# A transformer kernel: where the norm's spread, four lots of copies and a scaled product stand in their engines' queues

## What is computed

```python
mem_n = rmsnorm(mem, mem_norm)                       # 256 memory rows
for i in range(2):
    h = rmsnorm(x, norm_mix[i])                      # the mixer's norm
    ...                                              # projections, convolution or banded attention, memory attention
    x = x + concatenate([y_tok, y_mem]) @ w_out
    h = rmsnorm(x, norm_ffn[i])
    x = x + (silu(h @ w_gate[i]) * (h @ w_up[i])) @ w_down[i]
x = rmsnorm(x, final_norm)
...
kc = compress_blocks(k_c, ...); vc = compress_blocks(v_c, ...)   # blocks of 32 positions, stride 16, plus a place table
y_a = (o_a * silu(z_n)) @ w_nsa_o
y_b = (o_b * silu(z_r)) @ w_ret_o                    # o_b: retention, 4 heads, each normalised
merged = sigmoid(m_a) * y_a + sigmoid(m_b) * y_b
x = x + rms_norm(merged @ w_out, norm_post)
```

## Time and profile before

| | us |
|---|---|
| median of 3 runs | 1700.69 |
| lowest, highest | 1699.10, 1703.64 |
| the profiled execution | 1700.62 |
| its span | 1698.8 |
| PE busy in the span | 1634.9 |
| DVE, ACT, POOL busy | 871.4, 571.6, 152.9 |

### The profile page before, as it was taken

How to read it: one execution, slowest core, us unless ns; L and a number is a source line. 1 busy time by engine, 2 the same in 40 slices (tenths; PEclk the granted TensorE clock), 3 DMA queues, 4 the chain that set the end, 5 groups by cost and what they waited for, 6 DMA issues and landing times.

```text
span 1698.8 us, 20511 instructions
## 1 busy us (share of the span) xinstructions
PE 1634.9 (96%) x7720; PEld 1301.2 (77%) x7720; DVE 871.4 (51%) x1106; ACT 571.6 (34%) x962; POOL 152.9 (9%) x139
## 2 busy tenths in 40 slices
PE   7989999999999999879999999999999999999997
PEld 5867878888888876557888888887677777778886
DVE  5565544444423457655444443337476655446443
ACT  5332332222322335533222232322345542234222
POOL 3100100000000102120000001113211001000001
PEclk9999999999999999999999999999999999999999
DMA  5312622232332321122322232242111110232221
GB/s 211 125 62 88 142 89 98 99 97 90 120 102 97 103 71 35 33 73 97 99 99 96 91 125 85 97 186 89 51 63 50 50 63 31 75 98 95 99 100 74
DMA packets 44622, 154.88 MB, mean 91 GB/s; under 512 B 5230, under 2 KB 9999, under 8 KB 44047
## 3 DMA queue, kind: packets, MB, share of 16 engines
q1 hardware_dynamic: 40594, 146.92, 25.7%
q10 hardware_dynamic: 3964, 7.11, 1.9%
HBM read 149.55 MB, written 4.45 MB: 91 GB/s over the span
## 4 chain that ended last, share of the span: by engine, by line
PE 86%; DVE 8%; ACT 3%; issue 2%; POOL 1%; DMA 0%; DVEq 0%; SPq 0%; ACTq 0%; POOLq 0%
PE ps L1741 25%; PE ps L1743 24%; PE ps L1742 24%; DVE w_lo L1064 2%; PE ps L2095 1%; PE ps L2109 1%; PE ps L2131 1%; PE ps L2155 1%; POOL acc L590 1%; ACT w_hi L694 1%; PE ps L2196 1%; PE ps L2195 1%; PE ps L2194 1%; PE ps L1916 1%; DVE a_lo L1069 1%
## 5 line engine op out<-in xcount | busy, mean ns | idle before, releaser
L1741 PE MATMUL ps<-a_hi,w_hi 128*128 128x512 f32 (+1 forms) x1368 | 547.0, 400 | 16.4 <-DVE a_lo L1069 8.3
L1743 PE MATMUL ps<-a_hi,w_lo 128*128 128x512 f32 (+1 forms) x1368 | 535.0, 391 | 0.0
L1742 PE MATMUL ps<-a_lo,w_hi 128*128 128x512 f32 (+1 forms) x1368 | 534.8, 391 | 0.0
L1064 DVE TENSOR_TENSOR w_lo<-raw,w_hi 128x1024 fp32r<-128x1024 f32 (+4 forms) x262 | 324.2, 1237 | 253.6 <-ACT w_hi L694 248.5
L694 ACT ACTIVATE w_hi<-raw 128x1024 fp32r<-128x1024 f32 (+4 forms) x262 | 274.2, 1047 | 268.5 <-PE ps L1743 244.1
L1741 PEld LDWEIGHTS ps<-a_hi,w_hi 128*128 128x128 f32 (+1 forms) x1368 | 257.4, 188 | 82.0 <-issue 16.4
L1743 PEld LDWEIGHTS ps<-a_hi,w_lo 128*128 128x128 f32 (+1 forms) x1368 | 257.2, 188 | 55.8
L1742 PEld LDWEIGHTS ps<-a_lo,w_hi 128*128 128x128 f32 (+1 forms) x1368 | 257.6, 188 | 53.3 <-issue 1.9
L1090 DVE TENSOR_TENSOR tmp<-ps,rstd 128x512 f32<-128x512 f32 x121 | 83.4, 691 | 160.0 <-PE ps L1743 149.8
L1741 PE MATMUL ps<-g_hi,w_hi 128*128 128x512 f32 x352 | 136.9, 389 | 0.0
L1742 PE MATMUL ps<-g_lo,w_hi 128*128 128x512 f32 x352 | 136.9, 389 | 0.0
(11 more groups left out here) (271 smaller groups left out, 1749.4 us busy)
## 6 DMA issues: line engine op xcount, KB each, us to landing
raw<-w SPq DMA_DIRECT2D x135, 512.0 KB, 3.5
raw<-w8b SPq DMA_DIRECT2D x70, 512.0 KB, 3.5
raw<-w_down SPq DMA_DIRECT2D x32, 704.0 KB, 4.0
w<-cmp_w SPq DMA_DIRECT2D x2, 2048.0 KB, 10.9
raw<-w_out_first SPq DMA_DIRECT2D x8, 320.0 KB, 2.8
rel_scratch<-table ACTq DMA_DIRECT2D x1, 2298.0 KB
raw<-w_nsa_o SPq DMA_DIRECT2D x8, 256.0 KB, 2.5
out<-o_t SPq DMA_DIRECT2D x4, 512.0 KB, 2.7
```

Source lines behind the costliest of these rows:

```text
L1064: dve.tensor_tensor(w_lo[:, slot, 0:w], raw[:, raw_slot, 0:w], w_hi[:, slot, 0:w].bitcast(F32), ALU.subtract).then_inc(w_lo_ready, 1)
L1741: pe.matmul(o, wh, a_h, start=start and at == 0, stop=False)
L1742: pe.matmul(o, wh, a_l, start=False, stop=False)
L1743: ins = pe.matmul(o, wl, a_h, start=False, stop=stop and at == kt - 1)
```

## The change

Nothing is computed differently; every engine has the same instructions. What changes is where some of them stand:

- The spread of both mixer norms, of both feed-forward norms and of the memory norm stood ahead of a strip. It is now issued within that strip, behind its fourth tile (12 matmuls).
- On DVE, in both feed-forward layers and in the second mixer, the split's `w_lo` now stands ahead of `diagonal`.
- `windows_of` does four copies at a time, beside strips 188, 189, 190 and 191, in the order values, keys, values, keys.
- At a short strip DVE does `epilogue(n - 1)` ahead of the split (and ahead of the retention statistics), as at every other strip. ACT's order stays.

```diff
@@ vector, ffn @@
                         if first and j == 0:
+                            split(n + 2, w, 0, 2)
                             diagonal(v)
-                            split(n + 2, w, 0, 2)
                             dve.wait_ge(rstd_ready, v + 1)
@@ vector, second mixer @@
                 if n == N_QM1 + 2:
+                    split(n + 1, KT * P)
                     diagonal(V_MIX1)
-                    split(n + 1, KT * P)
                     dve.wait_ge(rstd_ready, V_MIX1 + 1)
@@ vector, third block @@
-            def windows_of(i):
+            def windows_of(i, g):
...
-                for g in range(2):
-                    for odd in range(2):
+                for odd in range(2):
...
-                if n >= N_SECOND + 3 and not short(n):
+                if n >= N_SECOND + 3:
                     epilogue(n - 1)
...
                 if N_SECOND < n < N_END - 1:
                     split(n + 1, width(n + 1))
-                if short(n):
-                    epilogue(n - 1)
...
-                if n in (N_SECOND + 5, N_SECOND + 6):
-                    windows_of(n - N_SECOND - 5)
+                if N_SECOND + 4 <= n < N_SECOND + 8:
+                    windows_of(*((1, 0), (0, 0), (1, 1), (0, 1))[n - N_SECOND - 4])
@@ tensor @@
+            def spread_beside(v, at):
+
+                if at == 3:
+                    spread(v)
...
-                if n == 4:
-                    spread(V_MIX0)
...
-                if n == 9:
-                    spread(V_MEM, 2)
...
-                        strip(n, mem_hi, mem_lo, bank_of(n), cols=NMEM)
+                        strip(n, mem_hi, mem_lo, bank_of(n), cols=NMEM,
+                              aside=(lambda at: spread(V_MEM, 2) if at == 3 else None) if n == 9 else None)
...
-                          aside=(lambda at, n=n: mem_beside(0, n, at)) if n > N_CONV else None)
+                          aside=(lambda at, n=n: mem_beside(0, n, at)) if n > N_CONV
+                          else (lambda at: spread_beside(V_MIX0, at)) if n == 4 else None)
@@ tensor, ffn @@
-                        if first and j == 2:
-                            spread(v)
...
-                              ready=(a_lo_ready, count) if first and j == 0 else None)
+                              ready=(a_lo_ready, count) if first and j == 0 else None,
+                              aside=(lambda at: spread_beside(v, at)) if first and j == 2 else None)
@@ tensor, second mixer @@
             def l1_beside(n, at, last):
+                if n == N_QM1 + 2:
+                    spread_beside(V_MIX1, at)
...
-                if n == N_QM1 + 2:
-                    spread(V_MIX1)
```

More of the change, by code:

```diff
@@ L1425, in windows_of @@
                 dve.wait_ge(small2_in, 16 * 5)
-                for g in range(2):
-                    for odd in range(2):
-                        of, to = slice(HD * g, HD * g + HD), slice(HD * odd, HD * odd + HD)
-                        src = (kcr, vcr)[i][of].rearrange("p (c l o) -> p l c o", l=CSTRIDE // 2, o=2)
-                        for w in range(2):
-                            ls = slice(CSTRIDE // 2 * w, CSTRIDE // 2 * (w + 1))
-                            place = pe2[of, i, odd, ls].unsqueeze(2).to_broadcast([HD, CSTRIDE // 2, NCMP])
-                            dve.tensor_tensor(windows[i][to, ls, g * NCMP:(g + 1) * NCMP],
-                                              src[:, :, w:w + NCMP, odd], place, ALU.add)\
-                                .then_inc(windows_ready, 1)
+                for odd in range(2):
+                    of, to = slice(HD * g, HD * g + HD), slice(HD * odd, HD * odd + HD)
+                    src = (kcr, vcr)[i][of].rearrange("p (c l o) -> p l c o", l=CSTRIDE // 2, o=2)
+                    for w in range(2):
+                        ls = slice(CSTRIDE // 2 * w, CSTRIDE // 2 * (w + 1))
+                        place = pe2[of, i, odd, ls].unsqueeze(2).to_broadcast([HD, CSTRIDE // 2, NCMP])
+                        dve.tensor_tensor(windows[i][to, ls, g * NCMP:(g + 1) * NCMP],
+                                          src[:, :, w:w + NCMP, odd], place, ALU.add)\
+                            .then_inc(windows_ready, 1)
             def cmp_maxima():
```

## The result

| us | before | changed |
|---|---|---|
| median | 1700.69 (1699.05 to 1703.64) | 1708.66 (1705.60 to 1710.61) |
| the profiled execution | 1700.62 | 1710.32 |
| its span | 1698.8 | 1708.5 |

The ratio is 1.0041, with a 95% interval of 1.0029 to 1.0054: 4.9 to 9.2 us slower. I had forecast 1702.5 and a range up to 1706.5. A second set of runs of the same kernel gave 1709.05 and a ratio of 1.0042. One execution in this set (2754.99) and one in another (2417.11, the product with the second mixer) took far longer than all others and are left out of every median here. The kernel before, in the sets of runs that were made beside the experiments, had medians from 1701.7 to 1703.0 (10 to 27 runs each, 1699 to 1705): the three runs shown ahead of the prediction were a little low.

A forecast was written before the change was run, and what follows sets the result against it. TensorE was taken as the bound, busy 1634.9 of 1698.8 us, leaving its waits and lower clock; about 10.3 lost and 8.4 won gave +1.9 on 1700.6, so 1702.5, range 1697.0 to 1706.5.

The forecast's parts named there:

- The slip in the feed-forward layers: Strip 39 and its like: later `rstd` delays `w_lo`, PE waits about 3.5 us; 2.73 lost per layer, 5.46 in all.
- The clock in these layers: Lower clock behind the waits of 3.5 us in both feed-forward layers: 1.4 each (0 to 1.7), together 2.8 lost.
- The first mixer: First mixer's norm: later `rstd` passes on 2.03 us, moving PE's wait at 55.90; 2.0 lost (1.3 to 2.7).
- The second mixer: Spread in the second mixer: PE's wait of 1.01 for `diag` becomes 0.5; 0.7 us gained (0.5 to 1.2).
- The short strips: Strips 221 to 229: five PE waits of 0.35 for `tmp` go; 3.0 us gained (2.0 to 3.2).
- the waits among the heads: Retention heads: waits of 1.57 at strip 216 and 1.42 at 218 go; net gains of 0.6 and 1.65 us.
- The windows: Copies in four lots end at 1180.2, so PE's compression product begins about 1180.7; 0.8 us gained (0 to 1.1).
- The stretch at 1452 gone: Low-clock stretch between 1452 and 1456 goes with the wait of 1.42 ahead of it; 1.6 us gained (0 to 1.7).
- The rival: Clock falls behind each new gap; at 1438 it costs 1.6, the stretch at 1452 only moves; total 1705.7, chance 0.15.

The follow-up runs named there:

- the product with the second mixer: Kernel before with the scaled product ahead of the split at short strips, and the second mixer's spread with its swap: 1696.2, ratio 0.9966.
- The feed-forward part alone: Kernel before with only the two feed-forward norms' spread behind the fourth tile, without the swap on VectorE: 1709.95, ratio 1.0056.
- the product alone: Kernel before with only the scaled product ahead of the split (and of the statistics) at every short strip: 1698.41, ratio 0.998.

## Why the prediction was wrong, step by step

- **The slip in the feed-forward layers** (2 x 2.73, PE's wait about 3.5): right to 0.05 us. The check that decided it was that PE was already late by 0.77 there, and that ACT's order, silu and `g_hi` ahead of `w_hi`, stayed.
- **The clock in these layers** (2.8): right in kind, though it fell behind only one of the two waits in the changed kernel's first trace. The feed-forward part alone costs 8.1 by medians and 9.5 by the ratio, of which 5.4 are waits, so 2.7 to 4.1 are clock. Some 0 to 1.3 short.
- **The first mixer** (+2.0): right by its waits. They stand at 48.74 and 54.00 and not at 55.90, where I had put them: the wait for the sums there is now covered by one for `w_lo`. The clock fell behind the wait of 2.15 in both traces of the changed kernel, and in none of the other three with that wait.
- **The second mixer** (-0.7): right; the new wait reads 0.35 for my 0.5.
- **The short strips** (-3.0) and **the waits among the heads** (-2.25, with one of about 2 before the transposes): right, though I hadn't named the copy that makes the wait 2.27.
- **The windows** (-0.8): wrong by 1.8. I took four copies to be half of a row of eight, at an end I estimated at 1180.2, and left out that the row of 6.39 is two rows: about four copies beside POOL and four free of it. The last lot as slow as the 6.39 row was my lower bound, and even that was too hopeful, since a lot of four meets as much of POOL's two instructions (2.6 us) as the row of eight did (2.7), and so loses nearly as much (4.0 us in all, not 3.2). They were there to be read, at 1172.95 and 1174.64. The 1.8 is by the traces; by its own runs this part cost nothing (-0.2), where I had 0.8 won.
- **The stretch at 1452 gone** (-1.6): the step that failed. I booked it as a cost of the kernel before that goes in full with its wait. It is a cost of some executions of it: of eleven traces with the wait of 1.42 three have it. And in half of the traces with the new wait of 2.27 another stands 14 us earlier. By these shares an estimate of the clock among the heads is 3/6 of 1.5 less 3/11 of 1.6, +0.3 where I had -1.6. The runs of the product alone bear this out: my terms for it come to -6.85 (3.0, 0.6, 1.65 and 1.6), and it measured -3.4 by the ratio, with every wait as worked out. The shares account for 1.9 of that difference; the rest is open. The rival had named this place and its price, at 0.15; by that rival the total was 1705.7.
- **The baseline.** I set the sum against the profiled execution because its time was the median of three. Its waits were typical, its clock wasn't at this place: it had lost nothing between 690 and 785, where nearly all others lost 1.6 to 4.5. Set against many runs of before (1701.8 and more), the change costs 7 (ratio) to 8.

Put together by the ratios: the feed-forward part 9.5 where I had 8.3, the rest of the change -2.7 where I had -6.4. Of that second miss of 3.7, 1.8 are the windows and 1.6 the stretch at 1452, both by the traces. **What stays open** is why the stretches between 690 and 785 cost more in the kernels with the slip (3.2 to 4.5 us in five unfilled traces) than in the ones without (0 to 4.3 in the others, mostly 1.6 to 2.7). The waits there are the same. With one trace or two for each kernel this may be chance, and it wasn't tried further.

## What to carry to other kernels

Moving work behind some tiles pays only at the engine that waits for it; where others hang on the work's result and PE is already late for theirs, each matmul of delay is paid in full, so look first at who hangs on it and whether they are late. In a sum for such an edit, waits repeated from one execution to the next to 0.05 us, but for a few, and may be added up; many stretches at half clock don't repeat, and should be entered as a price times the share of traces in which a gap of that length has one. A gap on TensorE can thus cost more than its length, and can be filled, where it can't be closed.

## What the runs showed of the hardware

- Useless products in a gap of 3.5 us kept the clock at 1.00 behind it, in both layers; the kernel's median was 2.4 us lower with them.
- A wait of 2.1 us had a half-clock stretch behind it in the first layer, which cost 1.6 us, and waits of 3.48 in the second layer were without one in two traces of four. The length of a gap doesn't decide alone.
- VectorE's copies of two inputs take 0.54 us each alone and 1.0 beside POOL's additions and products; POOL's product (line 653) took 1.3 alone, 1.5 beside the copies, and 2.25 in the kernel before at 1184.05, where it ran beside a `w_lo`.
